# Value rows of the third tile projected among the index products, with the sample's index scores in front of them

## The reference, cut to what matters

```python
u, q, k, v, qi, ki, wi = jnp.split(h @ w_in, SPLITS, axis=-1)     # v: 512 columns
# indexer: I[q,s] = sum_h w[q,h] relu(q_idx[q,h] . k_idx[s])
dots = jnp.einsum('bqhd,bsd->bqhs', qi, ki) * (IDX_DIM ** -0.5)
s = jnp.einsum('bqh,bqhs->bqs', w, jax.nn.relu(dots))
_, idx = lax.top_k(s, topk)              # 64 keys of each query
# attention over the chosen rows
out = softmax(q . k[idx] * HEAD_DIM ** -0.5) @ v[idx]
# state-space half
y = gelu(y_ssm);  y = y * sigmoid(y @ w_glu)
```

## Time and profile before

| | us |
|---|---|
| median of 3 runs | 1646.27 |
| lowest and highest | 1637.95, 1646.47 |
| the profiled execution | 1640.78 |
| its span in the profile | 1638.9 |
| TensorE busy | 1564.9 (95%) |
| VectorE busy | 1255.5 (77%) |
| ScalarE busy | 981.4 (60%) |

### The profile page before, as it was taken

One profiled execution on the slowest core, in us unless ns is written; L12 is line 12 of the kernel. 1 busy time (PEld: TensorE's weight loads), 2 busy tenths in 40 slices (PEclk: granted clock), 3 DMA queues, 4 the chain that ended last, 5 costly groups with the idle time before them and its releaser, 6 DMA issues.

```text
span 1638.9 us, 23592 instructions
## 1 busy us (share of the span) xinstructions
PE 1564.9 (95%) x7853; PEld 1267.7 (77%) x7853; DVE 1255.5 (77%) x1659; ACT 981.4 (60%) x1290; POOL 113.8 (7%) x156
## 2 busy tenths in 40 slices
PE   6998988899999579999999999999999999999998
PEld 5664554699999478888888888888888888888887
DVE  8978820255554679889989988888988988998986
ACT  5111442244443157777777777777777777777784
POOL 1377510000000000000000000000000000000000
PEclk9898979999999779999999999999999999999999
DMA  6401125334544419999989999998998998998992
GB/s 226 151 26 52 56 93 167 135 111 162 183 140 134 182 63 360 367 327 336 371 329 336 361 353 321 363 355 315 359 361 309 355 365 317 345 371 318 354 358 84
DMA packets 212887, 420.80 MB, mean 257 GB/s; under 512 B 10233, under 2 KB 56469, under 8 KB 212572
## 3 DMA queue, kind: packets, MB, share of 16 engines
q1 hardware_dynamic: 211542, 414.37, 70.3%
q10 hardware_dynamic: 622, 3.45, 0.5%
q0 software_dynamic: 672, 2.32, 0.4%
HBM read 417.50 MB, written 3.07 MB: 257 GB/s over the span
## 4 chain that ended last, share of the span: by engine, by line
PE 85%; DVE 3%; ACT 1%; issue 1%; DMA 1%; SPq 0%; ACTq 0%; DVEq 0%
PE bank L1252 19%; PE bank L1257 19%; PE bank L1256 19%; PE bank L1130 3%; PE bank L1133 3%; PE bank L1134 3%; PE bank L1207 2%; PE bank L1113 2%; PE bank L1277 1%; PE bank L1215 1%; PE bank L1145 1%; PE bank L1149 1%; PE bank L1148 1%; PE bank L860 1%; PE bank L823 1%
## 5 line engine op out<-in xcount | busy, mean ns | idle before, releaser
L2114 DVE TENSOR_TENSOR split<-raw_w,split 128x1024 fp32r<-128x1024 f32 x672 | 783.0, 1218 | 50.4 <-ACT split L1627 48.2
L1627 ACT ACTIVATE split<-raw_w 128x1024 fp32r<-128x1024 f32 x672 | 684.4, 1060 | 109.1 <-PE bank L1252 108.0
L1252 PE MATMUL bank<-split,xgr 128*128 128x512 f32 x896 | 359.2, 401 | 6.0 <-DVE split L2114 6.0
L1257 PE MATMUL bank<-split,xgr 128*128 128x512 f32 x896 | 354.4, 396 | 0.0
L1256 PE MATMUL bank<-split,xgr 128*128 128x512 f32 x896 | 354.2, 395 | 0.0
L1252 PEld LDWEIGHTS bank<-split,xgr 128*128 128x128 f32 x896 | 169.3, 189 | 43.8 <-DVE split L2114 6.4
L1257 PEld LDWEIGHTS bank<-split,xgr 128*128 128x128 f32 x896 | 169.1, 189 | 39.9
L1256 PEld LDWEIGHTS bank<-split,xgr 128*128 128x128 f32 x896 | 169.4, 189 | 37.5
L1252 PE MATMUL bank<-split,hbr 128*128 128x512 f32 x448 | 177.9, 397 | 0.0
L1257 PE MATMUL bank<-split,hbr 128*128 128x512 f32 x448 | 176.9, 395 | 0.0
L1256 PE MATMUL bank<-split,hbr 128*128 128x512 f32 x448 | 176.9, 395 | 0.0
(11 more groups left out here) (386 smaller groups left out, 1945.7 us busy)
## 6 DMA issues: line engine op xcount, KB each, us to landing
raw_w<-in_moe_gate SPq DMA_DIRECT2D x112, 1024.0 KB, 5.2
raw_w<-in_moe_up SPq DMA_DIRECT2D x112, 1024.0 KB, 5.9
raw_w<-in_moe_down SPq DMA_DIRECT2D x112, 1024.0 KB, 5.1
ring<-in_w_gate SPq DMA_DIRECT2D x11, 1024.0 KB, 5.0
ring<-in_w_up SPq DMA_DIRECT2D x11, 1024.0 KB, 7.3
ring<-in_w_down SPq DMA_DIRECT2D x8, 1408.0 KB, 6.4
ring<-in_w_in SPq DMA_DIRECT2D x5, 2048.0 KB, 9.5
ring<-in_w_out SPq DMA_DIRECT2D x2, 2048.0 KB, 8.1
```

Of the source, the lines that this page charges most:

```text
L1252: first = mm(out, hi, place[:, s, 0, cols], start=start, stop=False)
L1257: last = mm(out, hi, place[:, s, 1, cols], start=False, stop=stop)
L1627: A(place[:, s, 0, :], raw_w[:, at:at + BLOCK], ACT.Copy).then_inc(sem("high_ready"), 1)
L2114: TT(place[:, s, 1, :], raw_w[:, at:at + BLOCK], place[:, s, 0, :].bitcast(F32), ALU.subtract).then_inc(sem("low_ready"), 1)
```

## The change

The sample's product "sscore" moves from behind dot 8 to ahead of dot 0, and VectorE's addition of it from behind all dots to ahead of the first. The eight products of ("v", 2) no longer stand together between the logits of tiles 0 and 1; one each stands behind dots 4, 6, 8, 10, 12, 14, 16 and 18. They gather in bank 7, between "sscore" and "slogit", so the first of them waits until "sscore" has been read. ScalarE copies the result out behind the relu of dot 20. The slot of the unit "v" is now released by ("v", 1), not by ("v", 2).

```diff
@@ last_fill
     if unit == "v":
-        return (unit, TC - 1)
+        return (unit, 1)
@@ fill_order
-    f += logits(0) + [("v", 2)] + logits(1) + probs_T(0) + [("att", 0)] + logits(2)
+    f += logits(0) + logits(1) + probs_T(0) + [("att", 0)] + logits(2)
@@
-SAMPLE_FILLS = ["sdot", "sscore", "slogit"]
+SAMPLE_FILLS = ["sdot", "sscore", ("v", 2), "slogit"]
+VALUE_PARTS = {4 + 2 * c: c for c in range(C)}
@@ TensorE
+            emptied(pe, "sdot")
+            emptied(pe, "wbd")
+            mm(ps("sscore")[32:40, 0:SK], wbd[0:64, 0:NB], srelu[0:64, :],
+               start=True, stop=True).then_inc(full("sscore"), 1)
             for name in index_order():
...
-                if (t, h) == (1, 0):
-                    emptied(pe, "sdot")
-                    emptied(pe, "wbd")
-                    mm(ps("sscore")[32:40, 0:SK], wbd[0:64, 0:NB], srelu[0:64, :],
-                       start=True, stop=True).then_inc(full("sscore"), 1)
+                if H * t + h in VALUE_PARTS:
+                    c = VALUE_PARTS[H * t + h]
+                    if c == 0:
+                        emptied(pe, "sscore")
+                        unit_there("v")
+                    part = mm(ps(("v", 2))[0:TCN[2], :], h3[:, c, 2 * P:T], unit("v", 512)[:, c, :],
+                              start=(c == 0), stop=(c == C - 1))
+                    if c == C - 1:
+                        part.then_inc(full(("v", 2)), 1)
...
-                if name == ("logit", 1, 0):
-                    value_rows(2)
...
-            emptied(pe, "sscore")
+            emptied(pe, ("v", 2))
             slog = ps("slogit")
@@ ScalarE, in the loop over the dots
                       scale=HD ** -0.5).then_inc(free(("dot", t, h)), 1)
+                    if n == max(VALUE_PARTS) + 2:
+                        copy_rows(("v", 2), z3["v"])
...
             exps(0, 0, 4)
-            copy_rows(("v", 2), z3["v"])
             exps(0, 4, H)
@@ VectorE
             link(nc.vector.tensor_copy(sc[0:40, 2, :], init3[0:40, 2, :]))
+            filled(dve, "sscore")
+            TT(sc[32:40, 2, 0:SK], ps("sscore")[32:40, 0:SK], init3[32:40, 2, 0:SK], ALU.add).then_inc(free("sscore"), 1)
+            emptied(dve, "sscore")
             for name in index_order():
...
-            filled(dve, "sscore")
-            TT(sc[32:40, 2, 0:SK], ps("sscore")[32:40, 0:SK], init3[32:40, 2, 0:SK], ALU.add).then_inc(free("sscore"), 1)
-            emptied(dve, "sscore")
```

More of the change, by code:

```diff
@@ L1432, in copy_T, with copy_rows @@
                          ps(name)[:, :].rearrange("p (c t) -> p c t", c=4)[:, :, 0:n])
+            def copy_rows(name, dst):
+                t = name[1]
+                filled(act, name)
+                copy_out(name, dst[0:TCN[t], t, :], ps(name)[0:TCN[t], :])
             for t in range(TC):
```

## The result

The changed kernel takes 1648.9 us (median of 15 runs, 1644.69 to 1650.95), the kernel before on the same chip 1643.32 us (15 runs, 1637.95 to 1646.47): a ratio of 1.0033, 95% interval 1.0023 to 1.0043. It is slower by 5.6 us by the medians and 5.4 by the ratio, less than the half per cent by which faster and slower were to be told apart, but outside the uncertainty. I had forecast +0.3 us.

What follows compares the result with a forecast made beforehand. TensorE, busy 95% of the span, was taken to set the pace up to tile 1's first mask. That mask's -0.1 plus +0.4 for the clock gave +0.3 us on the median 1646.27: 1646.5 us, range 1636.5 to 1650.

Steps and rivals of the forecast that it cites:

- The size of the gain: Between the logits of tiles 0 and 1: 7.05 us leave TensorE, at most 4.7 us won because of `ssm_out`.
- M: Start of VectorE's first mask of tile 1, 210.01 us before; forecast at 209.9, a move of -0.1 us.
- Rival 4: At the first mask of tile 1: VectorE does not wait for `ssm_out`, all 7 us come through; 1643.9 us, chance 0.05.
- Ahead of ("y", 3): Index stage: sample product, six products of tile 2 and dots 5 to 15 make ("y", 3) end 3.05 us later.
- the 168.9 I had taken: Index stage: TensorE's clock rises 5.0 us after packed work begins, at 168.9; bounds 163.9 and 172.0.
- Behind ("y", 3): Third tile's dots with products 6 and 7: last relu ends 1.55 us later, and the GLU with it.
- value rows ... had 1.59 us of slack, so they are not last: Before the GLU: value rows of tiles 0 and 1 start 1.95 us later but do not hold it up.
- The clock, +0.4, bounds -1.3 and +2.3: Behind the first mask of tile 1: clock may fall earlier, +0.4 us; +2.3 if attention 0 doubles, -1.3 if the low spell ends early.
- The sign to look for: Behind the first mask of tile 1: a low clock from 209 to 220 would show the forecast wrong.
- This rule: Behind the first mask of tile 1: half clock unless activity lifts it; read strictly, a sum of +2.2 us.
- rival 3: Index stage: products run at half clock if it is not up by about 169.3; 1647.7 to 1650.0 us, chance 0.2.
- My dearest case, +3.7: Late clock in the index stage, +1.4 us, with attention 0 at half clock as well: +3.7 us.

Runs made afterwards that it cites:

- 2: Kernel before with one of tile 2's eight value products left at its old place and seven left out: 1639.96 us, ratio 0.9987.
- 3: Changed kernel with the block of eight products also back at its old place, so products and copy out are done twice: 1648.96 us, ratio 1.0037.
- experiment 4: Changed kernel with GpSimd's memset moved ahead of its first GELU product: 1645.76 us, ratio 1.0019.
- 7: Changed kernel with products 6 and 7 moved behind tile 1's value rows and the copy behind tile 1's exponentials: 1646.22 us, ratio 1.0021.
- 1: Kernel before with only the sample's score product and its addition moved ahead of the dots: 1644.59 us, ratio 1.0007.
- experiment 5: Changed kernel plus four products of 512 columns that nobody reads, ahead of attention 0: 1644.58 us, ratio 1.0006.
- 10: As 9, plus three more products nobody reads behind attention 1: 1636.44 us, ratio 0.9958.
- 8: Kernel before with tile 2's products split two, three and three over three TensorE waits, and the memset moved earlier: 1637.9 us, ratio 0.9963.
- 9: As 8, plus two products of 512 columns that nobody reads, ahead of attention 1: 1636.25 us, ratio 0.9958.

## Why the prediction was off

*The size of the gain, right.* At most 4.7 us, because `ssm_out` is next: 4.8 measured (experiments 2 and 3), with M behind GpSimd and no longer behind TensorE. Rival 4, that all 7 us come through, is excluded. What holds M there is not only the wait in the code: VectorE's own operation of 128x4 ahead of M ends with GpSimd's product too (209.86 + 1.84 = 211.70), so M could not have come earlier without that wait either.

*"Ahead of ("y", 3)", +3.05, measured +4.2.* The clock rose at 167.8, earlier than the 168.9 I had taken, which should have made it less. The term that was off is the pace: the last four products and the dots behind them took 174.90 - 168.50 = 6.40 us, four turns of 1.60, where I had 5.25. A turn of a product and two dots (one in the last turn) is dearer than 0.88 + 2 x 0.25 = 1.38, the sum of rows in which each kind stands in a row of its own: the product takes 0.97 to the start of the dots and the dots 0.63. My 0.25 came from dots of tile 2, with 16 rows of queries instead of 128. Why the turn is dearer was not tried. The pace is 1.15 of the missing 1.13; the start (-0.1), the first two turns (-0.1) and ("y", 3) (+0.2) cancel. Of the 4.2, up to 1.4 depends on when the clock happened to rise in the execution of before that one compares with.

*"Behind ("y", 3)", +1.55: right for the relu, wrong for who waits.* The last relu ended 185.53 - 179.37 = 6.16 after the first of these dots, before 4.63: +1.53. But the step "value rows ... had 1.59 us of slack, so they are not last" is false. The value rows started 4.54 after the first dot instead of 1.94, +2.6, where I had 1.95, and the GLU follows them one for one. I took a wait of TensorE's behind its own work for slack of that work, without asking what ended it: ScalarE's tanh stands behind the copy of the same value rows. Of the 1.05 us between 2.6 and 1.55, 0.4 is the false slack by my own number (1.95 against 1.55) and 0.65 the pace again. Together with the term before: 4.2 + 2.6 = 6.8 instead of 4.6, and M +2.05 instead of -0.1.

*The memset, not seen.* I moved M against GpSimd's product and did not look at what stands behind that product in GpSimd's queue: +1.3 us at the exponentials of tile 1.

*"The clock, +0.4, bounds -1.3 and +2.3": the largest error.* From the start of attention 0 to the key logits it is 249.95 - 217.91 = 32.04 us after and 243.60 - 214.90 = 28.70 before, +3.3, outside my bounds. I doubled attention 0 alone; the low spell also covered the logits of tile 2 and the transposes, and a second one began within attention 1 (4.90 us instead of 3.76). The reason I gave, that these stages wait for weights and data and not for columns alone, does not hold: attention 0 takes 1.97 us at full clock and 3.65 at half. How much of the 3.3 belongs to the change is known only roughly. The same difference is 1.3 to 3.6 in the kernels without the block ahead of M and without products that nobody reads (the change, 2, 4 and 7), and 0.0 and 1.4 in the two that keep the block (3 and 1). The sign to look for was named, a low clock "from 209 to 220"; it came from 215.6 to 225.8. The Trainium skill, page "TensorE: Matmul & The Clock Gate", section "Part 1: The HAM clock gate", says that half clock is the default and that activity lifts it. The trace agrees in direction: the clock fell where TensorE was busy 2.00 of 6 us, and with four more products there it stayed at 1.00 (experiment 5). This rule weighed against the change rightly.

2.05 + 1.3 + 3.3 = 6.7 is the delay in the profile; the medians say 5.6. The time lies where rival 3 had put it (1647.7 to 1650.0), yet not by its rule: the clock in the index stage was up well before 169.3, and M was late all the same. What rival 3 had right is attention 0 at half clock. The range of 1636.5 to 1650 held the time by luck and not by a mechanism well sized. It stood on the median of three runs of before, 1646.27, and fifteen runs have it at 1643.32. My dearest case, +3.7, ends at 1647.0 from there, below the 1648.9 measured: as a difference, +5.6 lies outside everything that I had priced.

Open: why +6.7 in the profile becomes +9.8 at its end and 5.6 in the medians. Several executions of each kernel would have to be profiled for that.

## What to carry to other kernels

A wait of an engine is not slack of the work ahead of it until one has read what ends that wait: if the releasing chain runs through a queue in which a consumer of that same work stands, delaying the work delays the end of the wait one for one. Work taken out of TensorE's path wins only up to the next wait, and may be paid for behind it with a lower clock. The better place for it is inside the waits: split over three of them, and with the memset out of VectorE's way, the same eight products left the kernel 0.37% faster than before instead of 0.33% slower.

## What the runs showed of the hardware

- A tiny operation can be held by another engine. VectorE's 128x4 took 0.17 us alone, 1.49 behind GpSimd's memset of 128x1152 (1.08 us), and 1.84 behind GpSimd's product; each time it ended within 0.1 us of GpSimd's. With the memset moved away it took 0.17 again (experiment 4). The Trainium skill, page "SBUF — State Buffer", section "SBUF: two separate sides", says that the two engines share one pair of ports by an exclusive lock. The trace agrees, with a memset too, which reads nothing. Which of the two took the ports first it does not settle: the memset's record begins 0.38 us behind VectorE's (213.59 against 213.21).
- TensorE can count as busy all the time and stand at 1.2 GHz: from 165.5 to 170.2 before at 0.50, and after, from 218 to 226, 8.00 of 8 us at 0.51. In experiment 5, with the four products ahead, the clock was at 1.00 in both stretches from 212 to 226.
- With the same products in the index stage, the clock rose 8.9 to 9.2 us behind VectorE's copy, from which delays are counted, in the profiles of before and of experiments 2 and 10, and 11.7 to 12.0 behind it in 8 and 9 (11.8 in 1); that made 1.3 to 1.4 us. A difference of that size in one trace is not yet an effect.
